# A two-layer diffusion backbone step: thirteen projection tiles moved into the latent attention, whose scores get one buffer of 1280 columns

## The reference

```python
h = rms_norm(x, p['norm1']) * (1 + sc1) + sh1
(na_q, na_k, na_v), pool_in, mla_q, ckv, kpe, (sq, sk, sv) = project_mixers(h, p)
o_na = neighbourhood_attention(na_q, na_k, na_v, c_na_k, c_na_v, p['na_rpb'])   # A
o_pool = multiscale_pool(pool_in, p['pool_w'], p['pool_scale'])                 # B
mk, mv = mla_expand_kv(ckv, kpe, p); ck, cv = mla_expand_kv(c_ckv, c_kpe, p)
o_mla = dense_attention(q, concat([mk, ck]), concat([mv, cv]))                  # C
o_swa = window_attention(axial_rope(sq), axial_rope(sk), sv, c_swa_k, c_swa_v, p['swa_sink'])  # D
x = x + g1 * (concat([o_na, o_pool, o_mla, o_swa]) @ p['w_out'])
x = channel_mlp(x, sh2, sc2, g2, p)
```

## Time and profile before

| | us |
|---|---|
| median of 3 runs (1759.56 to 1761.85) | 1760.49 |
| profiled execution, in all | 1765.45 |
| its span, first to last instruction | 1763.3 |
| TensorE busy | 1616.2 (92%) |
| DVE busy | 944.6 (54%) |
| ACT busy | 665.5 (38%) |
| POOL busy | 148.4 (8%) |

### The profile page before, as it was taken

One profiled execution on the slowest core, in us unless ns is written; L12 is line 12 of the kernel. 1 busy time (PEld: TensorE's weight loads), 2 busy tenths in 40 slices (PEclk: granted clock), 3 DMA queues, 4 the chain that ended last, 5 costly groups with the idle time before them and its releaser, 6 DMA issues.

```text
span 1763.3 us, 28315 instructions
## 1 busy us (share of the span) xinstructions
PE 1616.2 (92%) x11686; PEld 1494.5 (85%) x11686; DVE 944.6 (54%) x1480; ACT 665.5 (38%) x1045; POOL 148.4 (8%) x107
## 2 busy tenths in 40 slices
PE   5778997889999999999978789967999999999998
PEld 3655896579999999999958569945999999999998
DVE  3554336746665545554573543477565455544653
ACT  4455543753323322232243564256433222322231
POOL 1002202520000000000010040053000000000000
PEclk8798998999999999999988899989999999999999
DMA  9440343402222222223634205342212222222211
GB/s 310 145 148 1 46 132 111 134 25 73 72 72 72 72 73 96 72 73 99 203 105 134 84 1 105 107 150 61 67 55 74 88 78 72 72 72 72 78 66 60
DMA packets 150856, 160.14 MB, mean 91 GB/s; under 512 B 16390, under 2 KB 132808, under 8 KB 150728
## 3 DMA queue, kind: packets, MB, share of 16 engines
q1 hardware_dynamic: 150024, 158.13, 29.4%
q10 hardware_dynamic: 576, 0.16, 0.0%
q0 software_dynamic: 128, 0.05, 0.0%
HBM read 153.41 MB, written 4.65 MB: 90 GB/s over the span
## 4 chain that ended last, share of the span: by engine, by line
PE 78%; DVE 11%; ACT 6%; issue 2%; POOL 1%; DMA 1%; ACTq 0%; DVEq 0%; SPq 0%; POOLq 0%
PE ps L1545 32%; PE ps L1867 26%; PE ps L1618 12%; PE ps L1672 1%; PE ps L1525 1%; PE ps L1694 1%; PE ps L1641 1%; DVE extrema L1299 1%; PE ps L1571 1%; ACT pt_c L784 1%; POOL pr_a L748 1%; DVE extrema L1282 1%; PE ps L1661 1%; ACT pr_c L925 1%; DVE mod L1141 1%
## 5 line engine op out<-in xcount | busy, mean ns | idle before, releaser
L784 ACT ACTIVATE w_hi<-w_raw 128x2048 fp32r<-128x2048 f32 (+1 forms) x90 | 170.0, 1889 | 333.0 <-PE ps L1545 324.2
L1341 DVE SCALAR_TENSOR_TENSOR xT<-ps,mod,xT 128x128 f32<-128x128 f32 (+2 forms) x432 | 190.1, 440 | 195.6 <-PE ps L1545 183.7
L1128 DVE TENSOR_TENSOR w_lo<-w_raw,w_hi 128x2048 fp32r<-128x2048 f32 (+1 forms) x90 | 203.1, 2257 | 158.8 <-ACT w_hi L784 157.3
L1867 PE MATMUL ps<-xa_hi,w_hi 128*128 128x320 f32 (+1 forms) x1024 | 236.1, 312 | 0.0
L1867 PE MATMUL ps<-xa_lo,w_hi 128*128 128x320 f32 (+1 forms) x1024 | 235.2, 311 | 0.0
L1867 PE MATMUL ps<-xa_hi,w_lo 128*128 128x320 f32 (+1 forms) x1024 | 235.1, 311 | 0.0
L1545 PE MATMUL ps<-z_hi,w_hi 128*128 128x320 f32 x1024 | 233.9, 310 | 0.9 <-DVE xT L1341 0.9
L1545 PE MATMUL ps<-z_lo,w_hi 128*128 128x320 f32 x1024 | 233.3, 309 | 0.0
L1545 PE MATMUL ps<-z_hi,w_lo 128*128 128x320 f32 x1024 | 233.2, 309 | 0.0
L1618 PE MATMUL ps<-w_hi,h_hi 128*128 128x256 f32 (+1 forms) x560 | 167.4, 299 | 23.9 <-DVE h_lo L1195 16.2
L1100 ACT ACTIVATE z_relu<-z_relu,z_shift 128x128 f32<-128x128 f32 (+1 forms) x128 | 72.5, 566 | 306.7 <-DVE z_relu L1445 304.6
(11 more groups left out here) (235 smaller groups left out, 2144.0 us busy)
## 6 DMA issues: line engine op xcount, KB each, us to landing
w_raw<-in_mlp_w SPq DMA_DIRECT2D x64, 1024.0 KB, 5.3
ada_own<-in_w_ada SPq DMA_DIRECT2D x54, 512.0 KB, 4.6
w_raw<-in_w_in SPq DMA_DIRECT2D x14, 1024.0 KB, 8.0
ada_mix<-in_w_ada SPq DMA_DIRECT2D x21, 512.0 KB, 7.4
ada_room<-in_w_ada SPq DMA_DIRECT2D x15, 512.0 KB, 8.8
w_raw<-in_w_out SPq DMA_DIRECT2D x8, 768.0 KB, 5.3
ada_first<-in_w_ada SPq DMA_DIRECT2D x6, 512.0 KB, 9.1
x_in<-in_x_sample SPq DMA_DIRECT2D x1, 2048.0 KB, 8.8
```

The source lines that it names most:

```text
L784: do(nc.scalar.activation(out, in_, ACT.Copy), sem)
L1128: do(V.tensor_tensor(w_lo[:, n % 2, 0:w], w_raw[:, n % 2, 0:w], f32(w_hi[:, n % 2, 0:w]), ALU.subtract), w_lo_ready)
L1341: do(V.scalar_tensor_tensor(dst, src, gate[:, m:m + 1], dst, ALU.mult, ALU.add), sem if last else None)
L1867: last = M.matmul(bank(b + a_, s1 - s0), w[r][:, k, c:c + P], x[:, k, s0:s1], start=k == 0 and q == 0, stop=k == KC - 1 and q == 2)
```

## The change

- Scores of a pair in attention C are one block of 2n columns (1280 for a latent pair) in banks 0, 1 and half of 2. Head 0 is computed in parts of 512 and 128 columns, head 1 in parts of 384 and 256. A pair has one signal of its scores, one maximum instruction over both heads, one signal of its exponentials, and the next pair's scores wait for that.
- Bank 3 is for thirteen tiles (naq 2 to 4, nak, nav), each in a step j = 0 to 12 of the attention: on TensorE between scores and transposes, on ACT its copy between the exponentials and the copy of transposed probabilities. A tile in bank 3 waits for the copy of the one before it.
- split_hi of units 4, 5 and 6 goes into ACT's steps 0, 3 and 9, split_lo into DVE's steps 1, 5 and 11, ahead of that step's reciprocals and maxima.
- Behind the attention TensorE does swq's tiles, naq's and nak's transposes, then swkv's tiles. ACT squares naq, splits unit 7, and then copies swq's tiles with the two roots and nak's square between them.
- nav is staged where ada_own lies (st_nav), swq where the second half of c_q's room was (st_swq). ACT's waits for out_st1, nav_dma and out_st0 go; SP waits for out_st0 before it reloads ada_own.

```diff
-    def signals(i, h=1):
-        before = sum(2 if p[1] == "C" else 1 for p in pairs[:i])
-        return before + (h + 1 if pairs[i][1] == "C" else 1)
+    def signals(i):
+        return i + 1
+    in_c = [("naq", t) for t in range(2, NT)] + [(n, t) for n in ("nak", "nav") for t in range(NT)]
+    def proj_bank(i):
+        return 3 if proj[i][1:] in in_c else i % 2
...
+    st_nav = at("st_nav", ada_own_at, [P, NT, 256])
+    st_swq = at("st_swq", A0 + 1280, [P, NT, 256])
...
             if kind == "C":
-                return ps[:, 0:2048].rearrange("p (h n) -> p h n", h=2)[:, :, 0:n]
+                return ps[:, 0:2 * n].rearrange("p (h n) -> p h n", h=2)
...
                 load_weights(U + 10)
+                sp.wait_ge(out_st0, 48 * l + 16)
                 load_adas(48 * l + 32, range(OWN))
...
                     for h in range(2):
-                        act.wait_ge(max_ready, signals(i, h))
                         do(nc.scalar.activation(probs(i, pair)[:, h, :], scores(i, pair)[:, h, :], ACT.Exp,
                                                 bias=nb[:, i % 2, h:h + 1], scale=scale,
                                                 accum_out=lsum[:, i % 2, h:h + 1]),
-                           exp_done if h or kind == "C" else None)
+                           exp_done if h else None)
...
                     if kind_list == "C" and j < len(todo):
                         exps(*todo[j])
+                    if j in between:
+                        between[j]()
                     if 2 <= j < len(todo) + 2:
                         take_turned(*todo[j - 2])
...
-                attention(l, "C")
-                unit(3, "naq", lambda t: st[:, 0, t, :], 256, first=2, tiles=4, split=False)
-                unit(3, "naq", lambda t: st[:, 0, t, :], 256, first=4)
+                def filler(j):
+                    n, t = in_c[j]
+                    evacuate(l, n, t, places[n][:, t, :], 256)
+                    if j in (0, 3, 9):
+                        split_hi(U + {0: 4, 3: 5, 9: 6}[j])
+                attention(l, "C", {j: lambda j=j: filler(j) for j in range(len(in_c))})
                 square(l, "naq")
-                unit(4, "nak", lambda t: st[:, 1, t, :], 256, "naq")
+                split_hi(U + 7)
+                unit(6, "swq", lambda t: st_swq[:, t, :], 256, tiles=2, split=False)
+                root(l, "naq")
                 square(l, "nak")
+                unit(6, "swq", lambda t: st_swq[:, t, :], 256, first=2, tiles=3, split=False)
+                root(l, "nak")
+                unit(6, "swq", lambda t: st_swq[:, t, :], 256, first=3, split=False)
                 turn(l, "naq", 0)
                 turn(l, "naq", 1)
-                unit(5, "nav", lambda t: st[:, 0, t, :], 256, "nak")
                 turn(l, "nak", 0)
                 turn(l, "nak", 1)
-                act.wait_ge(out_st1, 16 * (l + 1))
-                unit(6, "swq", lambda t: st[:, 1, t, :], 256)
                 square(l, "swq")
-                act.wait_ge(nav_dma, 32 * (l + 1))
-                act.wait_ge(out_st0, 48 * l + 16)
                 unit(7, "swkv", lambda t: st[:, 0, t, :], 256, "swq")
...
-                    if kind == "C":
-                        for h in range(2):
-                            dve.wait_ge(scored, signals(i, h))
-                            do(V.tensor_reduce(mx[:, i % 2, h:h + 1], s[:, h, :], AX_X, ALU.max))
...
+                    if kind_list == "C" and j in (1, 5, 11):
+                        split_lo(45 * l + {1: 4, 5: 5, 11: 6}[j])
                     if kind_list == "C" and 1 <= j < len(todo) + 1:
                         reciprocals(*todo[j - 1])
...
                 attention(l, "C")
-                split_lo(U + 4)
-                split_lo(U + 5)
                 norm(l, "naq")
-                split_lo(U + 6)
+                split_lo(U + 7)
                 norm(l, "nak")
-                split_lo(U + 7)
                 split_lo(U + 8)
...
-                    if i >= 2:
-                        pe.wait_ge(p_read, i - 1)
+                    before = [j for j in range(max(0, i - 15), i) if proj_bank(j) == proj_bank(i)]
+                    if before:
+                        pe.wait_ge(p_read, before[-1] + 1)
...
                     if kind == "C":
+                        if i > todo[0][0]:
+                            pe.wait_ge(exp_done, signals(i - 1))
                         for h in range(2):
-                            if i > todo[0][0]:
-                                pe.wait_ge(exp_done, signals(i - 1, h))
...
-                attention(l, "C", {10: lambda: more_naq(2), 11: lambda: more_naq(3)})
-                project(l, U + 3, "naq", range(4, NT))
-                project(l, U + 4, "nak")
+                attention(l, "C", {j: lambda j=j: filler(j) for j in range(len(in_c))})
+                pe.wait_ge(exp_done, signals(pair_at[(l, "C", 3, 1)]))
+                project(l, U + 6, "swq")
                 pe.wait_ge(pt_ready, did["pair"])
                 pe.wait_ge(mix_lo, did["pair"])
                 pe.wait_ge(st_normed, norm_at(l, "naq") + 1)
...
-                project(l, U + 5, "nav")
...
-                project(l, U + 6, "swq")
                 project(l, U + 7, "swkv")
```

More of the change, by code:

```diff
@@ L426, in st_of @@
                 return k_st[:, :, :, :].rearrange("p t h w -> p (t h) w")
-            b = {"naq": 0, "nak": 1, "nav": 0, "swq": 1, "swkv": 0}[n]
             if n == "swkv":
-                return st[:, b, :, 0:128].rearrange("p t (h w) -> p t h w", w=HD)
-            return st[:, b, :, :].rearrange("p t (h w) -> p (t h) w", w=HD)
+                return st[:, 0, :, 0:128].rearrange("p t (h w) -> p t h w", w=HD)
+            x = {"naq": st[:, 0, :, :], "nak": st[:, 1, :, :], "swq": st_swq[:, :, :]}[n]
+            return x.rearrange("p t (h w) -> p (t h) w", w=HD)
         def sq_of(n):
@@ L861, in evacuate @@
                 act.wait_ge(p_done, i + 1)
-                src = bank(i % 2)
+                src = bank(proj_bank(i))
                 if n == "ukv":
@@ L908, in turn, with attention @@
                     copy(d_k[:, :], trans_view(i, NTOK + PAST), t_act)
-            def attention(l, kind_list):
+            def attention(l, kind_list, between={}):
                 todo = [(pair_at[(l, *p)], p) for kind in kind_list for p in attention_pairs(kind)]
@@ L1028, in _ @@
                     turn(l, "k", h)
-                attention(l, "C")
-                unit(3, "naq", lambda t: st[:, 0, t, :], 256, first=2, tiles=4, split=False)
-                unit(3, "naq", lambda t: st[:, 0, t, :], 256, first=4)
+                places = {"naq": st[:, 0], "nak": st[:, 1], "nav": st_nav, "swq": st_swq, "swkv": st[:, 0]}
+                def filler(j):
[4 more added lines that the diff above has]
+                attention(l, "C", {j: lambda j=j: filler(j) for j in range(len(in_c))})
                 square(l, "naq")
-                unit(4, "nak", lambda t: st[:, 1, t, :], 256, "naq")
+                split_hi(U + 7)
+                unit(6, "swq", lambda t: st_swq[:, t, :], 256, tiles=2, split=False)
+                root(l, "naq")
                 square(l, "nak")
+                unit(6, "swq", lambda t: st_swq[:, t, :], 256, first=2, tiles=3, split=False)
+                root(l, "nak")
+                unit(6, "swq", lambda t: st_swq[:, t, :], 256, first=3, split=False)
                 turn(l, "naq", 0)
                 turn(l, "naq", 1)
-                unit(5, "nav", lambda t: st[:, 0, t, :], 256, "nak")
                 turn(l, "nak", 0)
                 turn(l, "nak", 1)
-                act.wait_ge(out_st1, 16 * (l + 1))
-                unit(6, "swq", lambda t: st[:, 1, t, :], 256)
                 square(l, "swq")
-                act.wait_ge(nav_dma, 32 * (l + 1))
-                act.wait_ge(out_st0, 48 * l + 16)
                 unit(7, "swkv", lambda t: st[:, 0, t, :], 256, "swq")
@@ L1617, in project @@
                         for q, (p, r) in enumerate(((0, 0), (1, 0), (0, 1))):
-                            last = M.matmul(bank(i % 2)[:, 0:cols], x[p][:, k, :], w[r][:, k, :],
+                            last = M.matmul(bank(proj_bank(i))[:, 0:cols], x[p][:, k, :], w[r][:, k, :],
                                             start=k == 0 and q == 0, stop=k == kk - 1 and q == 2)
@@ L1633, in score @@
                     if kind == "C":
+                        if i > todo[0][0]:
+                            pe.wait_ge(exp_done, signals(i - 1))
                         for h in range(2):
[L1635 to L1636 removed]
                             head = 2 * hp + h
[L1638 to L1641 removed]
+                            parts = ((0, P),) if b is None else ((0, 512), (512, 640)) if h == 0 else ((0, 384), (384, 640))
+                            at0 = 0 if b is None else CTX
+                            for s, e in parts:
+                                last = M.matmul(out[:, h, s:e], c_q[0:QK, head, q], c_k[0:QK, head, at0 + s:at0 + e],
```

(15 more changed lines are left out.)

21 lines of the change are left out of this document (9 added, 12 removed).

## The result

The changed kernel takes **1796.75 us** (median of four runs, 1794.87 to 1798.45) against 1760.03 us for the kernel before (four runs, 1758.69 to 1761.85): ratio 1.021, 95% interval 1.019 to 1.0225, so 36.7 us slower. The forecast was 1790, with 1768 to 1806 as its range.

The account below looks back on a forecast made before the run. Bound by the ACT/DVE ring in attention, then TensorE in projections; a slower loop and late load make the stage 141.4 against 126.7 us: +14.7 per layer, +29.4, giving 1794.9, less 4.96 for the median, 1789.9; range 1768 to 1806.

Parts of the forecast that it names:

- first latent scores: Attention's start, counted from S, the first score: splits, then maximum and exponentials of pair 1 until 10.2; TensorE idles 3.1 us.
- clock in the first steps: Attention's start: TensorE's granted clock falls to the lower level after the idle time; 2.3 us added.
- steady step: Attention loop: scores 2.43, tile 2.9, transposes 1.28, exponentials 1.96, handovers 0.09 in a straight line, 8.66 us.
- step 9: Attention: its start after 10.2 + 2.3 + 15.5 + 43.45 = 71.4 us from the first score S.
- attention's end E: End of attention C: step 9's start at 71.4 plus 24.7 us for the rest, S + 96.1.
- from there to the end of swkv: Behind the attention: from the landing of unit 7's load (L) to the end of swkv's tiles, 31.3 us.
- stage: First score to last projection: 96.1 + 14 + 31.3 = 141.4 us against 126.7, +14.7 per layer.
- The ring: Attention: exponentials wait for transposes, next scores for both exponentials; steady loop loses 0.3 us per pair instead of gaining.
- the loop runs at TensorE's own pace: Rival, load still late: attention shorter by 7.8 us, +6.9 per layer, 1774 us; chance 0.15.
- The late load: Behind the attention: ACT's split of unit 7 (swkv's weights) waits for a load landing 14 us after E; TensorE stalls.
- interleaving pays: Rival: TensorE's 7.9 us sets the step, unit 7 comes in time; stage 117.3, -9.4 per layer, 1742; chance 0.10.
- the load is early enough: Rival, loop as forecast: swkv's tiles end at E + 31.2, +0.6 per layer, 1761.7, no change; chance 0.08.

Follow-up runs that it names:

- all_four: Changed kernel with unit 7's load early, its DVE split ahead of both norms, tiles behind transposes, maxima before splits, probabilities' copy before the tile's: 1744.11 us, ratio 0.9904.
- split_late: Changed kernel, load still late, with ACT's split of unit 7 behind swq's copies and both roots, DVE's behind nak's norm: 1774.51 us, ratio 1.0079.
- load_before: Kernel before, with only unit 7's load moved ahead of SP's wait for the attention's last values: 1761.71 us, ratio 1.0.
- all_but_load: Changed kernel with tiles behind transposes, maxima before splits, probabilities' copy before the tile's; load still late, unit 7's splits behind swq's copies and both norms: 1741.90 us.
- both_heads: Kernel before, with a pair's scores waiting for both exponentials of the pair before, no tiles moved: 1781.55 us, ratio 1.0111.
- load_early: Changed kernel with only unit 7's load moved ahead of SP's wait for the attention's last values: 1779.75 us, ratio 1.0117.

## Why the prediction was right, and where its sizes were off

The forecast was right in sign, mechanism and range, 6.8 us below the median. (The range's lower end does not follow from its terms: 1790 - 6 - 8 is 1776, not 1772.) Its own steps:

| Step (layer 0, us) | predicted | measured |
|---|---|---|
| first latent scores | S + 10.2 | S + 10.45 |
| clock in the first steps | +2.3 | about +4.8 |
| steady step | 8.66 | 8.37 |
| step 9 | S + 71.4 | S + 72.1 |
| attention's end E | S + 96.1 | S + 96.7 |
| load of unit 7 lands | E + 14 | E + 14.1 |
| from there to the end of swkv | 31.3 | 31.9 |
| stage | 141.4 | 142.7 |

**The ring.** Right: in steady steps the exponentials are released by the transposes and the next scores by the second exponential. The step was 0.29 too long, from 1.28 for transposes that take 1.10 until the exponential is released, and 1.96 for exponentials that take 1.85 until the scores start. Five steps give back 1.5 us, and the two small ones (7.49 for 7.76) another 0.5. The forecast counted a gap per pair, as a sign of too few buffers, on its side. The gap is there (0.73 us), but one score buffer alone does not make it: all_four has the same one buffer and no gap. It takes the order within the step as well. The rival in which the loop runs at TensorE's own pace, 7.9 us a step, did not come true in this order.

**The clock** took 2.5 more than I gave it. The first four latent steps were 9.15, 7.49, 9.97 and 9.93: against their neighbours at the full clock (7.49 for a small pair's transposes, 8.37) that is 1.66 + 1.60 + 1.56 = 4.8 us. This error and the 2.0 us of the ring nearly cancel, which is luck and not merit.

**The late load.** Right in place and in cause: DMA as releaser (12.79 us of ACT's wait), one matmul in 10.5 us, the lower clock behind it, and split_late shows that the wait's place in ACT's queue is the cause. The size was met too, but by other steps: in the forecast the load is issued at E + 8.8 and lands 5.2 us later, since the bias transfers took 7.93 us to issue before. They were issued in 4.4 us, so the load was issued at E + 5.3, and it took 8.8 us to land. Whether the sum holds because DMA was the limit, as the forecast argued, or by chance, these runs do not settle.

**The terms that were mis-sized.** In the trace the forecast was nearly met, +29.4 us against 30.2 between the two spans, but two errors cancel there. One is the base: "layer 1 runs the same code, so a sum per layer counts twice". The code is the same, the time before was not: layer 1's stage took 124.5 us, 2.2 less than layer 0's, since its lower clock was over after one pair instead of two. So the change cost 17.4 us there and 16.0 in layer 0, where the sum had 14.7 for each, 4.0 us too little in all. The other is that the sum leaves all outside the stages as it was, and it is 3.2 us shorter. That need not be the change's doing: in load_before, the kernel before with one load moved, the stages are 126.5 and 124.5 us again, and the rest is 1509.7, against 1512.1 in the profiled kernel before and 1509.0 in the changed one. That these two nearly cancel is luck. SP's new wait ahead of ada_own's loads cost next to nothing, as forecast: in the 76 us behind layer 0's stage TensorE waits 6.8 us for them, where it waited 6.0 before.

The largest error is the last term, from the trace to the median. I took off 4.96 us, because the profiled execution of the kernel before was that much above its median. The profiled execution of the changed kernel was 1.3 below its own. This makes 6.3 of the 6.8 us; it comes from which executions happened to be profiled, not from what the change does.

**The rival "interleaving pays"** was rejected since "the regime to be filled has no room". That was true of this order only. TensorE's own work is 7.9 us a step by the sum, which was 0.35 too high: with the tile behind the transposes a step takes 7.55, all of it busy, against 8.35 for a pair and a tile apart. The rival's price, a stage of 117.3 us and 1742, is what all_four (117.1 and 115.0; 1744.11) and all_but_load (1741.90) reach, each by five moves, in four queues and in three. By the Trainium skill's rule (Perfetto Trace Analysis, Optimization Strategy) interleaving regimes may help; these two runs agree, and the changed kernel itself shows that it can also cost.

**The rival "the load is early enough"** had 1761.7 and its experiment gave 1779.75. Its error was E + 31.2, for work alone (35.3 and 37.7 measured): TensorE waits 3.64 us for nak's norm, which the forecast had at 1.5 and this rival at nothing, and in layer 1 the lower clock follows. The tiles that covered the norm before are now in the attention.

What was not tried is two score buffers together with the tiles: the kernel gives the freed banks to the tiles.

## What to carry to other kernels

Work moved into a stage to fill an engine's idle time should sit behind the last thing that others wait for: here the same thirteen tiles cost 37 us or gained 15 to 20, by the order in the queues around them. Look in each queue for a wait on a transfer with unrelated work behind it: moving the waiting instruction back gave 22.2 us here, and the earlier load 17. And price both layers from their own rows, since a repeated stage need not take the same time twice, and put the median's distance from one profiled execution into the range, not into the sum.

## What the runs showed of the hardware that I had not expected

- With an edit that adds small waits, the lower level of TensorE's clock lasted for longer. In both_heads the first latent rounds, with gaps of 1.3 to 2 us, have a granted clock of 0.60 and 0.67; it is at 1.00 from 178 on. The columns are length, TensorE busy, granted clock, DMA share and GB/s.

```profile
138.00:160.00 22.00, 14.38 (x44) 0.60 0.00 0
160.00:170.00 10.00, 7.90 (x25) 0.67 0.00 0
170.00:178.00 8.00, 7.21 (x43) 0.80 0.00 0
178.00:200.00 22.00, 19.63 (x167) 1.00 0.01 2
```

  An edit that costs 0.1 us a round in the steady state thus cost 20.7 us in all. That the added gaps are what holds the clock down is argued from these rows; no run had the gaps at the full clock. The other reading, that the first rounds have too little other work to fill the ring's wait at any clock, is open too for the 4.2 us of idle time.
- SP's issue of the same eight transfers took 7.93 us with a load of a megabyte just ahead, 7.61 in load_before, also with one just ahead, 4.81 in load_early, 4.39 in the changed kernel and 4.12 in all_but_load, with none just ahead.
